# Hybrid layer with experts: z's gate by tanh, attention moved to z's banks, a mask in fp32r, experts' gate and up loaded whole

## The reference

```python
# first layer, cut
z, xbc, dt, q, k, v, gates = split(rmsnorm(x) @ w_in)
xs, B, C = silu(causal_conv4(xbc))              # 32 heads of 64, 4 groups
y = selective_scan(xs, dt, A, B, C) + d_skip * xs
y = rmsnorm(y * silu(z), per group of 512) * ssd_norm_g   # z: 512 tokens x 2048
s = y @ w_ssd_out
a = local_attention(rope(norm(q)), rope(norm(k)), v, sinks) @ w_attn_out
x = x + (sigmoid(ga) * a + sigmoid(gs) * s) @ w_out
# two of 64 experts for each token, hierarchical router
h = rmsnorm(x)
x = x + sum(weight_e * ((silu(h @ w_gate_e) * (h @ w_up_e)) @ w_down_e))
```

## Time and profile before

| what | us |
|---|---|
| median of 3 runs | 3135.32 (3130.08 to 3138.18) |
| profiled execution, its own time | 3132.55 |
| its span, first to last instruction | 3130.5 |
| PE busy in the span | 2749.1 (88%) |
| DVE busy | 1252.6 (40%) |
| ACT busy | 1034.8 (33%) |
| POOL busy | 904.7 (29%) |

### The profile page before, as it was taken

One profiled execution on the slowest core, in us unless ns is written; L12 is line 12 of the kernel. 1 busy time (PEld: TensorE's weight loads), 2 busy tenths in 40 slices (PEclk: granted clock), 3 DMA queues, 4 the chain that ended last, 5 costly groups with the idle time before them and its releaser, 6 DMA issues.

```text
span 3130.5 us, 40481 instructions
## 1 busy us (share of the span) xinstructions
PE 2749.1 (88%) x15814; PEld 2127.3 (68%) x15814; DVE 1252.6 (40%) x2335; ACT 1034.8 (33%) x2150; POOL 904.7 (29%) x620
## 2 busy tenths in 40 slices
PE   5999888889997888887888879999988787799999
PEld 3887666667874333333777759999987665577777
DVE  4654677762124122111345662233455555312112
ACT  3334333233223221112333443332244444332321
POOL 0001444421331032200222214654520000365553
PEclk8989999999998999999899979999998887699999
DMA  3321000032325999998111102323321010133332
GB/s 103 88 56 47 14 28 28 28 101 81 94 65 183 389 421 421 422 420 342 49 55 48 41 14 83 101 79 91 95 68 41 28 35 14 42 87 101 90 92 68
DMA packets 338559, 364.04 MB, mean 116 GB/s; under 512 B 16176, under 2 KB 295728, under 8 KB 330176
## 3 DMA queue, kind: packets, MB, share of 16 engines
q1 hardware_dynamic: 338368, 361.43, 33.6%
HBM read 359.29 MB, written 2.10 MB: 115 GB/s over the span
## 4 chain that ended last, share of the span: by engine, by line
PE 61%; DVE 13%; DMA 10%; ACT 7%; POOL 5%; issue 4%; SPq 0%; DVEq 0%; ACTq 0%; POOLq 0%
DMA early<-in_w_up_e 9%; PE bank L2156 5%; PE bank L443 5%; PE bank L445 5%; PE bank L444 5%; PE bank L2157 4%; PE bank L2158 4%; PE bank L1699 4%; PE bank L2587 4%; PE bank L2588 4%; PE bank L2589 4%; POOL split L2129 2%; DVE early L1128 1%; ACT split L2113 1%; DVE split L2132 1%
## 5 line engine op out<-in xcount | busy, mean ns | idle before, releaser
L2129 POOL TENSOR_TENSOR split<-keep,split 128x1024 fp32r<-128x1024 f32 x152 | 370.3, 2441 | 360.1 <-ACT split L2109 360.1
L2156 PE MATMUL bank<-x_hi,split 128*128 128x264 f32 (+1 forms) x1280 | 400.8, 313 | 12.6 <-POOL split L2129 8.3
L2157 PE MATMUL bank<-x_lo,split 128*128 128x264 f32 (+1 forms) x1280 | 395.3, 309 | 0.0
L2158 PE MATMUL bank<-x_hi,split 128*128 128x264 f32 (+1 forms) x1280 | 394.4, 308 | 0.0
L1699 PE MATMUL bank<-early 128*64 128x512 f32 x1024 | 234.7, 600 | 54.0 <-DMA early<-in_w_up_e 28.4
L2156 PEld LDWEIGHTS bank<-x_hi,split 128*128 128x128 f32 x1280 | 244.8, 191 | 40.7 <-issue 25.5
L2157 PEld LDWEIGHTS bank<-x_lo,split 128*128 128x128 f32 x1280 | 244.8, 191 | 10.2
L2158 PEld LDWEIGHTS bank<-x_hi,split 128*128 128x128 f32 x1280 | 243.9, 191 | 10.9
L2109 ACT ACTIVATE split<-keep 128x1024 fp32r<-128x1024 f32 x168 | 175.5, 1051 | 224.5 <-PE bank L2589 210.8
L1699 PEld LDWEIGHTS bank<-early 128*64 128x64 f32 x1024 | 81.8, 137 | 206.4 <-issue 180.0
L443 PE MATMUL bank<-x_hi,w_split 128*128 128x512 f32 x416 | 169.9, 409 | 20.0 <-DVE w_split L431 18.5
(11 more groups left out here) (460 smaller groups left out, 6370.3 us busy)
## 6 DMA issues: line engine op xcount, KB each, us to landing
early<-in_w_gate_e SPq DMA_DIRECT2D x128, 512.0 KB, 9.2
early<-in_w_up_e SPq DMA_DIRECT2D x128, 512.0 KB, 11.0
early<-in_w_down_e SPq DMA_DIRECT2D x64, 1024.0 KB, 11.4
early<-in_w_in SPq DMA_DIRECT2D x66, 512.0 KB, 3.7
keep<-in_mlp_w_in SPq DMA_DIRECT2D x64, 512.0 KB, 3.9
keep<-in_mlp_w_out SPq DMA_DIRECT2D x64, 512.0 KB, 3.7
keep<-in_a_w_qkv SPq DMA_DIRECT2D x24, 512.0 KB, 4.0
early<-in_w_ssd_out SPq DMA_DIRECT2D x16, 512.0 KB, 3.7
```

What stands on the lines that cost most here:

```text
L2129: e.tensor_tensor(lo, x, whole(hi), ALU.subtract).then_inc(*u.free(sig_, "lo", n))
L2156: e.matmul(o, hi[:, k, :], XH2[:, k, n0:n1], start=k == 0, stop=False, skip_group_check=True)
L2157: e.matmul(o, hi[:, k, :], XL2[:, k, n0:n1], start=False, stop=False, skip_group_check=True)
L2158: m = e.matmul(o, lo[:, k, :], XH2[:, k, n0:n1], start=False, stop=k == 7, skip_group_check=True)
```

## The change

z's gate becomes (tanh(z / 2) + 1) z, which is twice silu(z); the factor 2 is taken out behind the norm (1 / 512 becomes 1 / 2048 in the mean of squares, and the scaling multiplies by 0.5). Every second piece of z has its low half made by DVE. Identity and mask are copied once to fp32r. Attention takes its banks from `BR`. q k^T goes through both banks in turn. Gate and up of an expert are loaded whole, each into a buffer of its own, and used one after the other in products of 256 columns.

```diff
         def lo_on_pool(n):
-            return Z_FIRST <= n < G_FIRST or n >= G_FIRST and n % 2
+            return n >= Z_FIRST and n % 2
...
+        MASK = halves("mask", top[0], 2, 128)
+        top[0] += 256
+        IDENTR, NEGR = MASK[:, 0, :], MASK[:, 1, :]
...
-                        e.matmul(b.ap[:, :].rearrange("p (j n) -> p j n", j=4), C["ident"], bmid(C["negbig"], 4),
+                        e.matmul(b.ap[:, :].rearrange("p (j n) -> p j n", j=4), IDENTR, bmid(NEGR, 4),
...
-                    for bb in range(2):
-                        b = XR.take("qk", i, bb)
+                    bs = [BR.take("qk", i, bb) for bb in range(2)]
+                    for b in bs:
                         for s, n in b.before:
                             e.wait_ge(s, n)
-                        pr = cols(bb, 64)
-                        for hh in range(2):
-                            h = kv * 4 + 2 * hh + bb
-                            m = e.matmul(b.ap[:, hh * w:hh * w + w], QT[pr, h // 2, cols(n_, 128)], KT[pr, kv, k0:k0 + w],
+                    for hh in range(2):
+                        for bb in range(2):
+                            pr, h = cols(bb, 64), kv * 4 + 2 * hh + bb
+                            m = e.matmul(bs[bb].ap[:, hh * w:hh * w + w], QT[pr, h // 2, cols(n_, 128)], KT[pr, kv, k0:k0 + w],
...
-                        b = XR.take("pt", i, bb)
+                        b = BR.take("pt", i, bb)
...
-                    b = XR.take("pv", i)
+                    b = BR.take("pv", i)
...
         def mix_act(e):
+            table(e, SET_EXP_TANH)
+            e.wait_ge(*K.pe.to("rot", 11))
+            for i, name in enumerate(("ident", "negbig")):
+                e.activation(MASK[:, i, :], C[name], ACT.Copy).then_inc(*M.act.up("mask"))
...
                 if what == "z":
-                    z = ZR.of(i)
-                    e.wait_ge(*ZS.dve.to("low", i))
-                    e.activation(z.ap, z.ap, ACT.Exp, scale=-1.0).then_inc(*ZS.act.up("exp", i))
+                    z, b = ZR.take(i), BR.of("z", i)
+                    for s, n in z.before:
+                        e.wait_ge(s, n)
+                    e.wait_ge(*ZS.pe.to("mm", i))
+                    e.activation(z.ap, b.ap[:, 0:256], ACT.Tanh, scale=0.5).then_inc(*ZS.act.up("tanh", i))
...
                 if what == "z":
-                    b, z = BR.of("z", i), ZR.take(i)
-                    for s, n in z.before:
-                        e.wait_ge(s, n)
-                    e.wait_ge(*ZS.pe.to("mm", i))
-                    e.tensor_scalar(z.ap, b.ap[:, 0:256], -80.0, None, ALU.max).then_inc(*ZS.dve.up("low", i))
-                    e.wait_ge(*ZS.act.to("exp", i))
-                    e.tensor_scalar(z.ap, z.ap, 1.0, None, ALU.add).then_inc(*ZS.dve.up())
-                    e.wait_ge(*ZS.dve.now())
-                    e.reciprocal(z.ap, z.ap).then_inc(*ZS.dve.up())
-                    e.wait_ge(*ZS.dve.now())
-                    e.tensor_tensor(z.ap, z.ap, b.ap[:, 0:256], ALU.mult).then_inc(*b.free(ZS.dve, "silu", i))
+                    b, z = BR.of("z", i), ZR.of(i)
+                    e.wait_ge(*ZS.act.to("tanh", i))
+                    e.scalar_tensor_tensor(out=z.ap, in0=z.ap, scalar=1.0, in1=b.ap[:, 0:256], op0=ALU.add,
+                                           op1=ALU.mult).then_inc(*b.free(ZS.dve, "silu", i))
+                if what == "w":
+                    piece_lo(e, i, False)
...
-                        e.activation(SSQ, SSQ, ACT.Ln, bias=C["eps"], scale=1.0 / 512).then_inc(*O.act.up())
+                        table(e, SET_EXP_LN)
+                        e.activation(SSQ, SSQ, ACT.Ln, bias=C["eps"], scale=1.0 / 2048).then_inc(*O.act.up())
...
-                    for k0 in (0, 4):
+                    for kind, view in (("gate", wge), ("up", wue)):
                         for j in range(2):
-                            u = WX.take("up", 2 * i + j, k0)
+                            u = WX.take(kind, 2 * i + j)
                             for s, n in u.before:
                                 e.wait_ge(s, n)
-                            e.dma_start(u.ap[:, 0:1024], rowwise(wge[2 * i + j])[:, cols(k0 // 4, 1024)]).then_inc(*u.landing())
-                            u.again()
-                            e.dma_start(u.ap[:, 1024:2048], rowwise(wue[2 * i + j])[:, cols(k0 // 4, 1024)]).then_inc(*u.landing())
+                            e.dma_start(u.ap, rowwise(view[2 * i + j])).then_inc(*u.landing())
...
-                    for k0 in (0, 4):
-                        us = [WX.of("up", 2 * i + j, k0) for j in range(2)]
+                    for o, kind in ((0, "gate"), (256, "up")):
+                        us = [WX.of(kind, 2 * i + j) for j in range(2)]
...
-                        for k in range(4):
+                        for k in range(8):
                             for j in range(2):
-                                w = us[j].ap.rearrange("p (a k c) -> p a k c", a=2, k=4)
-                                m = e.matmul(b.ap[cols(j, 64), :].rearrange("p (a c) -> p a c", a=2), x.ap[:, k0 + k, cols(j, 64)], w[:, :, k, :],
-                                             start=k0 + k == 0, stop=k0 + k == 7, skip_group_check=True)
+                                m = e.matmul(b.ap[cols(j, 64), o:o + 256], x.ap[:, k, cols(j, 64)], wtile(us[j], 8, 256)[:, k, :],
+                                             start=k == 0, stop=k == 7, skip_group_check=True)
```

More of the change, by code:

```diff
@@ L13 @@
 AX = mybir.AxisListType
-SET_EXP_LN, SET_TRIG, SET_SILU, SET_SIGMOID = 6, 9, 18, 2
+SET_EXP_TANH, SET_EXP_LN, SET_TRIG, SET_SILU, SET_SIGMOID = 0, 6, 9, 18, 2
 NEG = -1.0e30
@@ L894, in mix_pe @@
             e.wait_ge(*K.dve.to("v", 15))
+            e.wait_ge(*M.act.to("mask"))
             for what, i in MIX:
@@ L946, in mix_pe @@
                     k0 = (n_ - 1) * 128 if n_ else 0
-                    for bb in range(2):
-                        b = XR.take("qk", i, bb)
+                    bs = [BR.take("qk", i, bb) for bb in range(2)]
+                    for b in bs:
                         for s, n in b.before:
                             e.wait_ge(s, n)
-                        pr = cols(bb, 64)
-                        for hh in range(2):
-                            h = kv * 4 + 2 * hh + bb
-                            m = e.matmul(b.ap[:, hh * w:hh * w + w], QT[pr, h // 2, cols(n_, 128)], KT[pr, kv, k0:k0 + w],
+                    for hh in range(2):
+                        for bb in range(2):
+                            pr, h = cols(bb, 64), kv * 4 + 2 * hh + bb
+                            m = e.matmul(bs[bb].ap[:, hh * w:hh * w + w], QT[pr, h // 2, cols(n_, 128)], KT[pr, kv, k0:k0 + w],
                                          start=True, stop=True, skip_group_check=True)
-                        m.then_inc(*M.pe.up("qk", i, bb))
+                            if hh:
+                                m.then_inc(*M.pe.up("qk", i, bb))
                 if what == "a1":
@@ L1028, in mix_act @@
                 if what == "a1" and ATT_UNITS[i][0]:
-                    b, p = XR.of("pt", i, 1), PT.of(i)
+                    b, p = BR.of("pt", i, 1), PT.of(i)
                     for s, n in p.before:
@@ L1035, in mix_act @@
                     n_, kv = ATT_UNITS[i]
-                    b = XR.of("pv", i)
+                    b = BR.of("pv", i)
                     e.wait_ge(*M.pe.to("pv", i))
@@ L1092, in mix_dve @@
                     for bb in range(2):
-                        b = XR.of("qk", i, bb)
+                        b = BR.of("qk", i, bb)
                         e.wait_ge(*M.pe.to("qk", i, bb))
@@ L1113, in mix_dve @@
                 if what == "a1":
-                    b, p = XR.of("pt", i, 0), PT.take(i)
+                    b, p = BR.of("pt", i, 0), PT.take(i)
                     for s, n in p.before:
@@ L1304, in out_dve @@
                             y = XS[:, c, cols(g, 512)]
-                            e.tensor_scalar(y, y, SSQ[:, c * 4 + g:c * 4 + g + 1], None, ALU.mult).then_inc(*O.dve.up("scaled", c, g))
+                            e.tensor_scalar(y, y, SSQ[:, c * 4 + g:c * 4 + g + 1], 0.5, ALU.mult, ALU.mult).then_inc(*O.dve.up("scaled", c, g))
                 if kind == "yT":
@@ L1691, in expert_pe @@
                     e.wait_ge(*F.dve.to("x", i))
-                    for k0 in (0, 4):
-                        us = [WX.of("up", 2 * i + j, k0) for j in range(2)]
+                    for o, kind in ((0, "gate"), (256, "up")):
+                        us = [WX.of(kind, 2 * i + j) for j in range(2)]
                         for u in us:
                             e.wait_ge(*u.landed())
-                        for k in range(4):
+                        for k in range(8):
                             for j in range(2):
-                                w = us[j].ap.rearrange("p (a k c) -> p a k c", a=2, k=4)
```

(8 more changed lines are left out.)

## The result

The changed kernel takes **3061.11 us** (median of 4 runs, 3060.34 to 3069.24), against 3135.05 us (median of 4). The ratio is 0.9771, 95% interval 0.975 to 0.9792: 74 us or 2.3% faster. The prediction was 3064 us.

The account below looks back on a forecast made before the run. DVE's in-order gate was taken to bound the mix, transfers the expert loop. Savings of 37.4 + 19.7 + 3 + 1 + 10 = 71 us off 3132.55, with 2.8 us added, gave 3064 us; range 3048 to 3082.

Parts of the forecast that it names:

- The iteration: Mix, iterations 4 to 14: 16.6 us each in place of 20.0, 37.4 us less over eleven.
- PE's own 14.7 us: Mix: PE's work in one new iteration at full clock, summed over decay, diagonal, state, attention and z products.
- the 0.7 us for the lower clock level: Mix: added to the 15.9 us of an iteration for PE's lower clock after pauses, which cost 1.4 us before.
- The tail: From iteration 15 to the output stage: 51.5 us in place of 71.25, 19.7 us less.
- Row halves in turn: Order of q k^T's K=64 products in attention: gives nothing, between 0 and 0.3 us an iteration.
- The table load: Output stage: one more load of 1.28 us in the chain that scales y, which starts earlier; net 1 us less.
- The experts: Expert loop: whole loads save 0.36 us an iteration in 28 of 32 iterations, 10 us less.
- a = 10 ns: Expert loads: price of one DMA packet beside its bytes; 576 packets fewer an iteration, 0.36 us over 16 engines.
- the prediction's second equation: Packet price, stretch 1230 to 1466 us: 3848 us of engine time = 22794 a + 99.20 b, packets and megabytes.
- The bank wait: Rival, mix: z waits behind DVE's copy, PE's lower clock stays, iteration 18.4 us, 3093 us; 16 in 100.
- the short products: Rival, expert loop: 256-column products cost PE 0.04 us a pair more, the experts gain nothing, 3076 us; 10 in 100.
- the weight loads: Rival, expert loop: each of 32 pairs adds its 0.17 us exposed, 118 us slower, 3192 us; 4 in 100.

Follow-up runs that it names:

- g1: The kernel before with the new gate alone (ACT's tanh, one fused DVE instruction, table loads, factor 0.5): 3082.37 us, ratio 0.9839.
- g2: The changed kernel with the old gate put back (clamp, exp, add, reciprocal, multiply): 3122.62 us, ratio 0.997.
- m1: The changed kernel with the mask product in fp32 again: 3072.02 us, ratio 0.9805.
- c2: c1 with z's second piece split before the iteration's scan work from iteration 6 on: 3034.11 us, ratio 0.9686.
- r1: The changed kernel with q k^T in the old order, two heads of one row half, then two of the other: 3061.88 us, ratio 0.9773.
- q1: The changed kernel with gate and up loaded in four transfers each, 2 KB a packet: 3078.66 us, ratio 0.9828.
- x1: The changed kernel with attention's banks taken from the scan's ring again, z alone on its own: 3064.41 us, ratio 0.9788.
- p1: The changed kernel with all of z's low halves on POOL again: 3058.44 us, ratio 0.9767.
- e1: The changed kernel with the experts' loads and products as before: 3073.21 us, ratio 0.9807.
- c1: The changed kernel with both copies of the turned probabilities made by ACT: 3050.77 us, ratio 0.974.

## Why the prediction was right, and where its sizes were off

The sum came out because errors in opposite directions cancelled, and that is luck. The mix and the stretch behind it gave 5.3 and 1.5 us more than foretold; the experts gave 5 less, and the first four iterations and the output stage 1 less each. The mechanism of the mix, from which 66 of the 71 us come, held.

*The iteration* (16.6 foretold, 16.1 measured). Each link held: DVE's gate was the limit (g1, g2), the mask showed nearly in full (m1), z's bank came to wait for DVE's copy (16 us of waits), and PE's own 14.7 us was the floor (c2). The term too large was the 0.7 us for the lower clock level: with short pauses the granted clock averaged 0.98, and 2% of 16.1 is 0.3 us. Without the clock the sum was 15.9, and 16.1 less 0.3 is 15.8. In the sum, DVE's low halves at 1.24 us were right for six of eight; two took 2.06.

*The tail.* 19.7 foretold, 21.2 measured, with a wait of 3.3 us for z's last piece where 3.7 was worked out.

*Row halves in turn* gave nothing (r1), as the 1.14 us of eight instructions had said. *The table load* and the earlier start of the scaling chain together gave nothing: output stage and routing took 332.9 us in the profile before and 333.0 after (331.3 to 337.3 over all profiles). Neither was tested by itself.

*The experts.* This is the mis-sized term: "a = 10 ns" a packet and 0.36 us an iteration; measured 4.9 ns, so 576 x 4.9 / 16 = 0.18 us, times 28 the 5 us that the loop lost. The step that failed was to take busy time of the queue for time that passes. A share over 100% said already that one packet's time overlaps the next; it falls to 100.8% with 8 KB packets and rises to 103.7% with 2 KB ones, so part of what a packet costs in the records costs nothing on the clock. Solved with busy time, the three rows under q1 give 9.1 ns, near the prediction's 10; solved with the time that passed, 4.9. To put 3776 for 3848 in the prediction's second equation would not have mended it (it gives 10.4 ns), because the first one, of a stretch in which the queue is 30% busy, is of busy time as well. Only stretches in which the queue never rests give the price: their rates against packets and bytes.

*The rivals.* The bank wait arose but did not decide; the short products cost PE next to nothing (3.67 us a group in place of 3.65); the weight loads were not exposed. Two edits of the change remain without a shown worth: the banks (x1: some 3 us above the other executions with the same mix) and the low halves (p1: nothing). Left open: why e1's total rose by 6 us more than its loop, and c2's fell by more than its mix.

## What to carry to other kernels

Add up, engine by engine, what an iteration must do and what it waits for in its own program; the sum of the pacing engine (14.7 us here) tells how far a change can go, and the wait that follows the one removed can be read off the same rows. An engine that works in order has its free places where it waits for another: DVE's low half, moved there in c2, took 10 us off the iterations of c1, while moving it to another engine (p1, on the changed kernel) gained nothing. The two runs start from different kernels, so this compares them only roughly. Before a difference of a few us is read as an effect, look at executions that share the code in question. A gain on an engine that doesn't pace shows only once the pacing one is relieved (g2 against m1).

## What the runs showed of the hardware that was not expected

A DMA packet costs 4.9 ns of an engine's time beyond its bytes, though the records' busy time says 9 to 10. A DVE subtraction of 1024 columns takes 1.22 us by itself and 2.06 us with POOL's L1159 beside it for 0.98 us. And pauses on PE cost twice: in iterations 4 to 14 the granted clock averaged 0.90 with all but the gate, 0.93 before, 0.98 in the changed kernel and 1.00 in c2, in which PE hardly pauses.
